# Activation tiles of a streaming encoder step at a pitch of 320 columns instead of 288, with six small buffers put into shared places

## The chip, the cores and the metric

The kernel runs on one core of one Trainium2 chip. The metric is the device time of one execution in microseconds (us). Smaller is better.

## The reference: what is computed

One layer of a streaming encoder for two request groups that share weights: a prompt of 256 tokens and a sample of 32 tokens with a cache of 128 past ones, 288 tokens in all. The model width is 2048, the FFN width 5504. Everything is float32.

```python
xp = xp + 0.5 * swiglu_ffn(xp, *ffn1)             # the same for the sample group, xs
op, sp = mixer_prompt(rmsnorm(xp, g1), *lw)       # z = h @ W_in, three attention groups, concat @ W_out
xp = xp + op
xp = xp + 0.5 * swiglu_ffn(xp, *ffn2)
# swiglu_ffn(x) = (silu(h @ w_gate) * (h @ w_up)) @ w_down, with h = rmsnorm(x, g)
```

The mixer's groups are A (12 heads over 4 key heads, the keys chosen by a lightning indexer: per query the top quarter of the keys by a weighted sum of relu(q_idx . k_idx)), B (10 heads over 2 key heads, window 128, sinks) and C (10 heads, clipped relative bias). Keys and values are also returned as caches.

## The kernel before, in words

**Tiling.** Activations lie transposed: 128 partitions carry 128 of the features, and the 288 tokens lie along the free dimension. A tile of 128 x 288 float32 is thus 1152 bytes in each partition. `h_hi` and `h_lo` (16 tiles each) hold the normalized input, `gu_hi` and `gu_lo` (15 tiles each) a third of the gated FFN values, `o_hi` and `o_lo` (16 tiles each, in the same place as `gu`, at another time) the attention output. These six are the "streamed" or right-side tensors: the moving operands of the large products.

**Precision.** Each float32 product is made of three products in the type float32r: `hi` and `lo` are the upper and the remaining part of a number, of activations as of weights. In `products` three matmuls per tile k go to one PSUM bank:

```python
pe.matmul(out, w_hi[b][:, k, :], hi, start=(k == first_k), stop=False)     # L594
pe.matmul(out, w_hi[b][:, k, :], lo, start=False, stop=False)              # L595
mm = pe.matmul(out, w_lo[b][:, k, :], hi, start=False, stop=(k == last_k)) # L596
```

Each of them also loads its 128 x 128 weight tile (LDWEIGHTS). A *strip* is all k of one output tile of 128 features.

**Phases.** `plan_phases` puts the strips in order. For each FFN, three times: *up* (30, 28 and 28 strips of 16 tiles; gate and up in turn) and *down* (16 strips of 15, 14 and 14 tiles). Between the two FFNs: *prep* (11 strips: index queries, keys and values), *cb* (20 strips with the attention of groups C and B between them), *a* (6 strips with attention A) and *wo* (16 strips). That makes 4,976 steps of k, so 14,928 large matmuls. All strips run one after another on TensorE. SyncE brings each strip's weights into `raw` (two buffers), ScalarE makes `w_hi` (L1049), VectorE makes `w_lo` (L1360), one strip ahead. VectorE reads the finished products from PSUM (L1384, L1720), ScalarE and VectorE make the next right side (L1266, L1685).

**Norms.** The sum of squares of x for an RMS norm is gathered in `sumsq` (VectorE, cleared at L1696, added to at L1367) from `sqx` (ScalarE, L1055), multiplied with a matrix of means (L641) and its root taken into `sd_x` (L1066). This happens three times: at the start, in the last *down* of the first FFN, and in *wo*.

**Attention buffers.** `kt_c` holds the keys of one pair of C heads (288 new, 128 cached): GpSimd places the cached ones (L1849), VectorE the new ones (L1414), GpSimd's queue stores the new ones to the output (L1898, L1899, semaphore `k_out`). `sq`, `z_k`, `p_t` serve attention too. `vec_t5` holds T5 bias vectors until they are stored in DRAM near the start. `idx_acc` holds the index sums for three blocks of queries.

**Places.** On-chip tensors lie one behind another in the order in which they are created. In the laid-out program before, these are the first bytes of a partition's share: `h_hi` 35,136 (137 x 256 + 64), `h_lo` 53,568 (209 x 256 + 64), `gu_hi` and `o_hi` 121,152 (473 x 256 + 64), `gu_lo` 138,432 (540 x 256 + 192), `o_lo` 139,584 (545 x 256 + 64). The weight tensors `w_hi` and `w_lo` all start at 64 past a multiple of 256, and their tiles are 512 bytes apart. As 1152 is 4.5 x 256, successive tiles of a right side lie alternately at 64 and at 192 past a multiple of 256.

Of the kernel before, what the change touches and what calls it, by code (L numbers as in the profile page):

```python
# [13 lines left out]
F32R = mybir.dt.float32r  # L14

P = 128
HD = 64
CHUNK = 64
H_A, KV_A, H_IDX, H_B, KV_B, H_C = 12, 4, 8, 10, 2, 10
# [6 lines left out]
VEC = 3 * P  # L26
# [87 lines left out]
def encoder_step(nc, x, cak, cav, caki, cbk, cbv, cck, ccv, w_in, w_out, qk_norm, sinks, c_bias, t5_bias,  # L114
                 w_gate, w_up, w_down, onehot,
                 yt, pak, pav, paki, pbk, pbv, pck, pcv, sak, sav, saki, sbk, sbv, sck, scv):
    T_P, T_S = pav.shape[2], sav.shape[2]
    D = w_out.shape[0]
    PAST = cav.shape[2]
    D_FF = w_gate.shape[1]  # L120
    NT = T_P + T_S
    DT, FT = D // P, D_FF // P
# [5 lines left out]
    thirds = [p.more["size"] for p in phases if p.name == "up"][:3]  # L128


    ctx = ExitStack()
    with ctx:
        def sb(name, shape, dt=F32, scope=ctx):
            return scope.enter_context(nc.sbuf_tensor(name, shape, dt))

        def sem(name):
            return ctx.enter_context(nc.semaphore(name))
# [2 lines left out]
        x_room = sb("gains_and_x", [P, 3 * DT + DT * NT])  # L140
        g_cols = x_room[:, 0:3 * DT]
        xT = x_room[:, 3 * DT:3 * DT + DT * NT].rearrange("p (k n) -> p k n", n=NT)
        h_hi = sb("h_hi", [P, DT, NT], F32R)
        h_lo = sb("h_lo", [P, DT, NT], F32R)
        raw = [sb(f"raw{s}", [P, 16, P]) for s in range(2)]
        w_hi = [sb(f"w_hi{s}", [P, 16, P], F32R) for s in range(2)]
        w_lo = [sb(f"w_lo{s}", [P, 16, P], F32R) for s in range(2)]
# [2 lines left out]
            below_second = sb("below_second", [P, 2, NT], F32, scope)  # L150
            raw_second = [sb(f"raw_second{s}", [P, 16, P], F32, scope) for s in range(2)]
        with ExitStack() as ffn_scope:
            gu_hi = sb("gu_hi", [P, thirds[0], NT], F32R, ffn_scope)
            gu_lo = sb("gu_lo", [P, thirds[0], NT], F32R, ffn_scope)
        o_hi = sb("o_hi", [P, 16, NT], F32R)
        o_lo = sb("o_lo", [P, 16, NT], F32R)

        ident = sb("ident", [P, P])
        mean_d = sb("mean_d", [P, P])
# [4 lines left out]
        sink_rows = sb("sink_rows", [P, 2, 5])  # L164
        neg_sinks = sb("neg_sinks", [P, 2, 5])
        rstd = sb("rstd", [P, NT])
        sumsq = sb("sumsq", [P, NT])
        sqx = sb("sqx", [P, NT])
        sd_x = sb("sd_x", [P, NT])
        table_first = sb("table_first", [P, 3])  # L170
        warm = gu_hi[:, 0:2, :].rearrange("p k n -> p (k n)")[:, 0:512]

        KEYS = T_P + PAST + T_S
        kt_a = sb("kt_a", [P, 2, KEYS])
# [20 lines left out]
        z_k = sb("z_k", [P, NT])  # L195
# [3 lines left out]
        sq = sb("sq", [P, NT])  # L199
# [2 lines left out]
        sq_wide = [sq_room[:, at:at + WIDE] for at in (0, NT, NT + WIDE)]  # L202
        sq_set = [t[:, 0:NT] for t in sq_wide]
        key_hi, key_lo = o_hi[:, 5, :], o_lo[:, 5, :]
        sd = sb("sd", [P, NT + 12])
        rinv = sb("rinv", [P, NT])
        v_c = sb("v_c", [P, 4, P])
        kt_c = sb("kt_c", [P, KEYS])
        vec_t5 = sb("vec_t5", [H_A + H_B, VEC])

        with ExitStack() as scope:
            t5_rows = sb("t5_rows", [T5_BUCKETS, H_A + H_B], F32, scope)
# [1 line left out]
        s_buf = [sb(f"s_buf{s}", [P, 2, T_P]) for s in range(2)]  # L214
        s_buf += [z_prep[:, 0:2, 0:T_P], z_prep[:, 2:4, 0:T_P]]
        p_t = [sb(f"p_t{r}", [P, 4, P]) for r in range(3)]
        bias_rev = [sb(f"bias_rev{s}", [P, 2, T_P]) for s in range(2)]
        idx_acc = [sb(f"idx_acc{r}", [P, n]) for r, n in enumerate((2 * P, P, PAST + T_S))]
        a_mask = [sb(f"a_mask{r}", [P, n]) for r, n in enumerate((2 * P, P, PAST + T_S))]
        nmax = [sb(f"nmax{s}", [P, 2]) for s in range(2)]  # L220
        snk = [sb(f"snk{s}", [P, 2]) for s in range(2)]
# [83 lines left out]
        k_out = sem("keys_stored")  # L305
# [16 lines left out]
        def x_piece(i):  # L322

            return [at for at, (s, _) in enumerate(FIRST) if s == 0].index(i)

        def first_no(i):

            return sum(k.stop < DT for _, k in FIRST[:i + 1])
# [99 lines left out]
        VOUT_PREP, KOUT_PREP = len(vout_no), len(kout_no)  # L428
# [587 lines left out]
        def _(act):  # L1016
# [114 lines left out]
            def prep_items(step):  # L1131
                for it in PREP_ITEMS.get(step, []):
                    if it[0] == "n":
                        z, done = {"ka0": (0, 6), "ka1": (1, 7), "kb": (8, 10)}[it[1]]
                        squares(z_prep[:, z, :], phase["prep"].n0 + done)
                        deviation(misc_no[it], norm_no[it])
                    elif it[0] == "v":
                        v, cols, _, _, _ = v_place(it[1])
                        place_v(misc_no[it], v, cols)
                    elif it[0] == "s":  # L1140
                        set_deviation(misc_no[it], 0, True, (0, 1))
                    elif it[0] == "w":
                        act.wait_ge(m_done, misc_no[it] + 1)
                        act.activation(w_tok[:, 0:2, :], misc_bank(misc_no[it])[:, 0:2 * H_IDX].rearrange("p (t c) -> p t c", t=2), ACT.Copy)
                        act.activation(w_tok[0:T_S, 2, :], misc_bank(misc_no[it])[0:T_S, 2 * H_IDX:3 * H_IDX], ACT.Copy).then_inc(m_free, 1)
                    elif it[0] == "i":
                        u = it[1]
                        r, _ = idx_units[u]
                        act.wait_ge(iq_done, u + 1)
                        if u >= 2:  # L1150
                            act.wait_ge(iacc, 2 * u - 2)
                        m, n = ROWS[r], NKEY[r]
                        for c in range(2):
                            a = act.activation(s_buf[u % 2][0:m, c, 0:n], psum[2 + u % 2 * 2 + c][0:m, 0:n], ACT.Relu)
                        a.then_inc(irelu, 1)
# [180 lines left out]
        def _(dve):  # L1336
            steps = [0]

            def link(ins):

                steps[0] += 1
                ins.then_inc(dve_link, 1)
                dve.wait_ge(dve_link, steps[0])
# [300 lines left out]
            for ph in phases:  # L1644
# [42 lines left out]
                elif ph.name in ("down", "wo"):  # L1687
# [5 lines left out]
                    if h_after:  # L1693

                        dve.wait_ge(m_done, [0, 1, 2][index])
                        link(dve.memset(sumsq[:, :], 0.0))  # L1696

                    final = ph.next is None
# [38 lines left out]
                elif ph.name == "prep":  # L1737
# [10 lines left out]
                    n = ph.n0 + 4  # L1748
# [275 lines left out]
```

## Time and profile before

| | |
|---|---|
| Time, median of 3 runs | 2085.09 us (2084.61 to 2085.61) |
| Span of the profiled execution | 2083.5 us (the page gives the span alone; the median of the timed runs is 1.6 us above it) |
| TensorE matmuls busy | 2077.8 us, 15,805 instructions |
| TensorE weight loads busy | 2057.7 us, 15,805 instructions |
| VectorE, ScalarE, GpSimd busy | 1169.9, 846.7, 88.8 us |
| Granted TensorE clock | 1.000 (mean) |

A matmul's duration in the profile is the time from its start to its modelled end, and it overlaps the next one; what a matmul costs is the distance from its start to the next one's start.

### The profile page before, as it was taken

How to read it: one execution, taken by the hardware profiler on the slowest of the kernel's cores; microseconds unless marked ns; L12 is line 12 of the kernel's file. 1: busy time of each engine (PE TensorE's matmuls, PEld its weight loads, DVE VectorE, ACT ScalarE, POOL GpSimd, SP SyncE). 2: the span in 40 equal slices, each digit the busy share in tenths (PEclk: the TensorE clock that was granted, in tenths of full speed). 3: DMA queues.
4: the chain of work that ended last, by engine and by line, in shares of the span. 5: the costliest groups of instructions: out<-in, count | busy, mean ns of one | idle time of the engine just before them, and what ended most of it. 6: DMA issues, size and time to landing. Idle time of an engine off the chain costs nothing.

```text
span 2083.5 us, 41883 instructions
## 1 busy us (share of the span) xinstructions
PE 2077.8 (100%) x15805; PEld 2057.7 (99%) x15805; DVE 1169.9 (56%) x1790; ACT 846.7 (41%) x1290; POOL 88.8 (4%) x140
## 2 busy tenths in 40 slices
PE   9999999999999999999999999999999999999999
PEld 8999999999999999999999999999999999999999
DVE  7554445554455556588879755555445554455544
ACT  6333333333333344345558544333333333333332
POOL 0000000000000000022432000000000000000000
PEclk9999999999999999999999999999999999999999
DMA  7444555444544545544443454544445444545554
GB/s 256 161 161 158 170 169 169 161 159 160 175 156 167 165 152 175 176 142 154 150 151 112 146 165 163 169 166 158 169 159 166 165 166 159 169 161 165 165 180 140
DMA packets 101274, 339.96 MB, mean 163 GB/s; under 512 B 12149, under 2 KB 16293, under 8 KB 101200
## 3 DMA queue, kind: packets, MB, share of 16 engines
q1 hardware_dynamic: 95856, 329.41, 47.7%
q0 software_dynamic: 2960, 7.45, 1.3%
q10 hardware_dynamic: 2400, 2.33, 0.3%
q8 instruction: 36, 0.59, 0.1%
q14 instruction: 22, 0.18, 0.0%
HBM read 334.45 MB, written 5.28 MB: 163 GB/s over the span
## 4 chain that ended last, share of the span: by engine, by line
PE 98%; DVE 1%; DMA 0%; ACT 0%; SPq 0%; issue 0%; DVEq 0%; ACTq 0%
PE bank L594 32%; PE bank L596 31%; PE bank L595 31%; PE bank L681 1%; PE bank L714 1%; PE bank L696 1%; PE bank L658 0%; DMA raw<-in_w_ffn_gate 0%; PE bank L896 0%; PE bank L698 0%; DVE w_lo L1360 0%; ACT w_hi L1049 0%; DVE rstd L1378 0%; PE bank L717 0%; PE bank L719 0%
## 5 line engine op out<-in xcount | busy, mean ns | idle before, releaser
L594 PE MATMUL bank<-h_hi,w_hi 128*128 128x288 f32 x3344 | 994.3, 297 | 0.9 <-DVE w_lo L1617 0.8
L595 PE MATMUL bank<-h_lo,w_hi 128*128 128x288 f32 x3344 | 986.5, 295 | 0.0
L596 PE MATMUL bank<-h_hi,w_lo 128*128 128x288 f32 x3344 | 983.3, 294 | 0.0
L1360 DVE TENSOR_TENSOR w_lo<-raw,w_hi 128x1024 fp32r<-128x1024 f32 x634 | 729.7, 1191 | 208.1 <-ACT w_hi L1049 207.6
L1049 ACT ACTIVATE w_hi<-raw 128x1024 fp32r<-128x1024 f32 x634 | 617.5, 1022 | 328.0 <-PE bank L596 325.5
L594 PEld LDWEIGHTS bank<-h_hi,w_hi 128*128 128x128 f32 x3344 | 626.7, 187 | 5.8 <-DVE w_lo L1617 2.1
L596 PEld LDWEIGHTS bank<-h_hi,w_lo 128*128 128x128 f32 x3344 | 629.8, 188 | 0.0
L595 PEld LDWEIGHTS bank<-h_lo,w_hi 128*128 128x128 f32 x3344 | 628.0, 188 | 0.2
L594 PE MATMUL bank<-gu_hi,w_hi 128*128 128x288 f32 x1376 | 407.0, 296 | 0.0
L595 PE MATMUL bank<-gu_lo,w_hi 128*128 128x288 f32 x1376 | 406.8, 296 | 0.0
L596 PE MATMUL bank<-gu_hi,w_lo 128*128 128x288 f32 x1376 | 406.4, 295 | 0.0
L596 PEld LDWEIGHTS bank<-gu_hi,w_lo 128*128 128x128 f32 x1376 | 259.6, 189 | 0.0
L595 PEld LDWEIGHTS bank<-gu_lo,w_hi 128*128 128x128 f32 x1376 | 259.6, 189 | 0.0
L594 PEld LDWEIGHTS bank<-gu_hi,w_hi 128*128 128x128 f32 x1376 | 259.4, 188 | 0.0
L1266 ACT ACTIVATE gu_hi<-gu 128x288 f32 (+1 forms) x86 | 38.2, 445 | 391.5 <-DVE gu L1682 391.5
L1720 DVE SCALAR_TENSOR_TENSOR gains_and_x<-bank,gains_and_x 128x288 f32 (+1 forms) x96 | 43.9, 457 | 201.4 <-PE bank L596 200.4
L1262 ACT ACTIVATE g_sig<-g_act 128x288 f32<-128x288 f32 x86 | 38.2, 444 | 283.9 <-DVE g_act L1384 283.9
L1384 DVE TENSOR_TENSOR u_act<-bank,rstd 128x288 f32<-128x288 f32 x86 | 39.3, 457 | 165.1 <-PE bank L596 165.0
L1384 DVE TENSOR_TENSOR g_act<-bank,rstd 128x288 f32<-128x288 f32 x86 | 39.4, 458 | 117.9 <-PE bank L596 117.8
L1685 DVE TENSOR_TENSOR gu_lo<-gu,gu_hi 128x288 f32 (+1 forms) x86 | 39.4, 458 | 67.8 <-ACT gu_hi L1266 67.8
L594 PE MATMUL bank<-o_hi,w_hi 128*128 128x288 f32 x256 | 75.9, 297 | 0.0
L595 PE MATMUL bank<-o_lo,w_hi 128*128 128x288 f32 x256 | 75.6, 295 | 0.0
(198 smaller groups left out, 985.8 us busy)
## 6 DMA issues: line engine op xcount, KB each, us to landing
raw<-in_w_ffn_gate SPq DMA_DIRECT2D x168, 512.0 KB, 4.5
raw<-in_w_ffn_up SPq DMA_DIRECT2D x168, 512.0 KB, 4.5
raw<-in_w_ffn_down SPq DMA_DIRECT2D x96, 512.0 KB, 3.7
raw<-in_w_in SPq DMA_DIRECT2D x74, 512.0 KB, 4.6
raw<-in_w_ffn_down SPq DMA_DIRECT2D x64, 384.0 KB, 4.2
raw<-in_w_out SPq DMA_DIRECT2D x32, 512.0 KB, 4.5
raw<-in_w_ffn_down SPq DMA_DIRECT2D x32, 448.0 KB, 4.3
bias_rev<-bias_vectors POOLq DMA_DIRECT2D x11, 256.0 KB, 4.6
```

Source lines behind the costliest of these rows:

```text
L594: pe.matmul(out, w_hi[b][:, k, :], hi, start=(k == first_k), stop=False)
L595: pe.matmul(out, w_hi[b][:, k, :], lo, start=False, stop=False)
L596: mm = pe.matmul(out, w_lo[b][:, k, :], hi, start=False, stop=(k == last_k))
L681: mm = pe.matmul(bank_s[c][:, b * T_P:b * T_P + NKEY[r]], q[half, FULL[r]], kt[half, KEY0[r]:KEY0[r] + NKEY[r]], start=True, stop=True)
L696: mm = pe.transpose(bank_t[b][:, o:o + P], s_buf[slot][:, c, kc * P:(kc + 1) * P], ident[:, :])
L1049: act.activation(w_hi[b][:, k, :], raw_tile(ph, j, s)[:, k, :], ACT.Copy).then_inc(hi_rdy, 1)
L1262: act.activation(g_sig[:, :], g_act[:, :], ACT.Silu).then_inc(sig_rdy, 1)
L1266: act.activation(gu_hi[:, j, :], gu[:, :], ACT.Copy).then_inc(guh_rdy, 1)
L1360: dve.tensor_tensor(w_lo[b][:, k, :], raw_tile(ph, j, s)[:, k, :], w_hi[b][:, k, :].bitcast(F32), ALU.subtract)\
L1384: return dve.tensor_tensor(dst, (early_bank(n) or bank_w[b])[rows, cols], rstd[rows, cols], ALU.mult)
L1685: dve.tensor_tensor(gu_lo[:, j, :], gu[:, :], gu_hi[:, j, :].bitcast(F32), ALU.subtract).then_inc(gul_rdy, 1)
L1720: dve.scalar_tensor_tensor(dst, src[:, 0:NT], factor, xT[:, d, :], ALU.mult, ALU.add)\
```

## The change

The right sides get a pitch of `TILE = -(-NT // 64) * 64`, that is 320 columns (1280 bytes) instead of 288. The matmuls still read 288 columns each, and columns 288 to 319 of a tile are never read by a product. This takes 8,192 bytes more of each partition. Room comes from putting other buffers together: `sqx` becomes `sq`, `sd_x` becomes `z_k`, `sumsq` becomes the first 288 columns of `kt_c`, `vec_t5` a part of `p_t[1]`, and the first two `idx_acc` parts of `p_t[0]` (6,528 bytes less). One wait is added: before `sumsq` is cleared in *wo*, VectorE waits until all stores of keys have landed. No instruction is added or removed otherwise, and the instructions' order stays.

```diff
+        def right_side(name, tiles, scope=ctx):
+            room = sb(name, [P, tiles, TILE], F32R, scope)
+            return room[:, :, 0:NT], room
+
+        TILE = -(-NT // 64) * 64
-        h_hi = sb("h_hi", [P, DT, NT], F32R)
-        h_lo = sb("h_lo", [P, DT, NT], F32R)
+        h_hi, _ = right_side("h_hi", DT)
+        h_lo, _ = right_side("h_lo", DT)
...
-            gu_hi = sb("gu_hi", [P, thirds[0], NT], F32R, ffn_scope)
-            gu_lo = sb("gu_lo", [P, thirds[0], NT], F32R, ffn_scope)
-        o_hi = sb("o_hi", [P, 16, NT], F32R)
-        o_lo = sb("o_lo", [P, 16, NT], F32R)
+            gu_hi, gu_room = right_side("gu_hi", thirds[0], ffn_scope)
+            gu_lo, _ = right_side("gu_lo", thirds[0], ffn_scope)
+        o_hi, _ = right_side("o_hi", 16)
+        o_lo, _ = right_side("o_lo", 16)
...
-        sumsq = sb("sumsq", [P, NT])
-        sqx = sb("sqx", [P, NT])
-        sd_x = sb("sd_x", [P, NT])
-        warm = gu_hi[:, 0:2, :].rearrange("p k n -> p (k n)")[:, 0:512]
+        warm = gu_room[:, 0:2, :].rearrange("p k n -> p (k n)")[:, 0:512]
...
+        sqx = sq
+        sd_x = z_k
-        vec_t5 = sb("vec_t5", [H_A + H_B, VEC])
+        sumsq = kt_c[:, 0:NT]
...
+        vec_t5 = p_t[1][0:H_A + H_B, 0:VEC // P, :].rearrange("p k n -> p (k n)")
+        first_rows = p_t[0][:, 0:3, :].rearrange("p k n -> p (k n)")
-        idx_acc = [sb(f"idx_acc{r}", [P, n]) for r, n in enumerate((2 * P, P, PAST + T_S))]
+        idx_acc = [first_rows[:, 0:2 * P], first_rows[:, 2 * P:3 * P], sb("idx_acc2", [P, PAST + T_S])]
...
                         dve.wait_ge(m_done, [0, 1, 2][index])
+                        if ph.name == "wo":
+                            dve.wait_ge(k_out, 32 * (KOUT_PREP + 5))
                         link(dve.memset(sumsq[:, :], 0.0))
```

## Rows read from the trace of the kernel before

**Rows 1.** The page's first part: busy time by engine.
```profile
PE 2077.8 (100%) x15805; PEld 2057.7 (99%) x15805; DVE 1169.9 (56%) x1790; ACT 846.7 (41%) x1290; POOL 88.8 (4%) x140
```
**Rows 2.** The waits of TensorE: total us, times, longest.
```profile
PE bank L905 <- DVE gu_hi L1594: 1.7, 1, 1.7
PE bank L594 <- DVE w_lo L1617: 0.8, 2, 0.6
PE bank L698 <- DVE z_prep L1477: 0.2, 1, 0.2
```
**Rows 3.** Windows of six phases: length, PE busy (instructions), clock, DMA share, GB/s.
```profile
202.40:298.10 95.70, 95.70 (x723) 1.00 0.50 167
298.10:477.30 179.20, 179.20 (x1347) 1.00 0.49 162
477.30:566.90 89.60, 89.60 (x674) 1.00 0.50 167
...
1447.70:1543.40 95.70, 95.70 (x723) 1.00 0.50 166
...
1812.10:1991.30 179.20, 179.20 (x1346) 1.00 0.49 163
1991.30:2080.80 89.50, 89.50 (x672) 1.00 0.50 166
```
**Rows 4.** Timeline of TensorE in an up phase: start us, us, instruction.
```profile
599.78 0.29 PE L594 MATMUL bank<-h_hi,w_hi 128*128 128x288 f32 x1
599.91 0.29 PE L595 MATMUL bank<-h_lo,w_hi 128*128 128x288 f32 x1
600.05 0.29 PE L596 MATMUL bank<-h_hi,w_lo 128*128 128x288 f32 x1
600.18 0.30 PE L594 MATMUL bank<-h_hi,w_hi 128*128 128x288 f32 x1
...
600.58 0.29 PE L594 MATMUL bank<-h_hi,w_hi 128*128 128x288 f32 x1
...
600.98 0.30 PE L594 MATMUL bank<-h_hi,w_hi 128*128 128x288 f32 x1
...
603.78 0.29 PE L594 MATMUL bank<-h_hi,w_hi 128*128 128x288 f32 x1
```
**Rows 5.** The same in a down phase.
```profile
499.78 0.30 PE L594 MATMUL bank<-gu_hi,w_hi 128*128 128x288 f32 x1
...
500.31 0.30 PE L595 MATMUL bank<-gu_lo,w_hi 128*128 128x288 f32 x1
500.45 0.29 PE L596 MATMUL bank<-gu_hi,w_lo 128*128 128x288 f32 x1
500.59 0.29 PE L594 MATMUL bank<-gu_hi,w_hi 128*128 128x288 f32 x1
...
502.19 0.29 PE L594 MATMUL bank<-gu_hi,w_hi 128*128 128x288 f32 x1
```
**Rows 6.** The tile mean_d: duration ns min/median/max, first and last start us.
```profile
L641 PE MATMUL bank<-sumsq,mean_d x6: 405/406/406, 34.9 to 1261.6; 128*128 128x288 f32 x6
```
**Rows 7.** Timeline of TensorE around the first norm product.
```profile
34.87 0.65 PE L641 MATMUL bank<-sumsq,mean_d 128*128 128x288 f32 x2
```
**Rows 8.** The tiles kt_c and sumsq: durations as above, first and last start.
```profile
L1849 POOL COPY kt_c<-kc_cache x5: 422/2304/2462, 858.5 to 1075.4; 128x128 f32 x3, 128x128 f32<-128x128 f32 x2
L1899 POOL DMA_DIRECT2D out<-kt_c x5: 537/540/540, 959.4 to 1088.9; - x5
...
DMA to landing us min/median/max: 4.7/5.0/5.5
...
L1696 DVE MEMSET sumsq<- x2: 298/298/298, 748.0 to 1168.1; 128x288 f32 x2
```

## The prediction

> **What bounds the kernel now.** I began with busy time by engine [rows 1]: TensorE is busy for 2077.8 of the 2083.5 us of the span, VectorE for 56% of it, ScalarE for 41%. A busy share of 100% doesn't prove a bound, since matmuls overlap in this view, so I went on to TensorE's waits [rows 2]: they sum to 2.7 us in the whole span. Neither weights, nor right sides, nor free banks come late, apart from the first 50 us. Only two things can then move the time: the distance between starts of the 14,928 large matmuls, or a new wait long enough to reach TensorE.
>
> The windows by phase give that distance [rows 3]. An up phase of 28 strips has 28 x 16 x 3 = 1344 large matmuls and takes 179.2 us: 133.3 ns each (the two or three further instructions in the row's count are neighbours cut by the window's ends). A down phase with 14 tiles has 672 and takes 89.6 us: again 133.3. A down phase with 15 tiles has 720 and takes 95.7 us: 132.9. The second FFN's rows repeat this. So 14,928 x 133.3 ns = 1,990 us of the span is this one number. The other 93 us are start, attention and end.
>
> At the full clock, 288 columns at one per 2.4 GHz cycle are 120 ns; the row's 133.3 ns are 320 cycles. That 13.3 ns are missing, and that 320 is the new pitch, makes one suspicious that the chip charges for a rounded-up tile. The question of the case is whether the place of a tile decides this.
>
> **The change part by part.** *The pitch.* Every large matmul still reads 288 columns and its own weight tile, so no work goes away by count. What changes is the place at which a read starts. Before, tiles lie alternately 64 and 192 bytes past a multiple of 256. With 1280 = 5 x 256 every tile keeps the place of its tensor's first one. The added bytes ahead of each tensor (2,048 for each of `h_hi` and `h_lo`, so 4,096 before `gu` and `o`) are multiples of 256. So `h_hi`, `h_lo`, `gu_hi`, `o_hi` and `o_lo` start at 64 past as before, and `gu_lo`, behind 15 x 1280 = 19,200 bytes = 75 x 256, moves from 192 to 64. After the change all tiles lie at 64 past a multiple of 256. None lies on a multiple of 128 or of 256, neither before nor after. The change makes the places equal; it doesn't align them.
>
> And 64 past is not a new place: half of the tiles have it before. If it were cheaper or dearer than 192 past, the trace would show it. In an up phase all three matmuls of a tile k read from one kind of place, the next three from the other. The starts of L594 lie 0.40 us apart from tile to tile: 599.78, 600.18, 600.58, 600.98, and ten tiles after the first 603.78, which is 4.00 us later [rows 4]. No two neighbours differ by more than the row's rounding of 0.01 us, which is 3 ns for one matmul. In a down phase hi and lo of a tile lie at different places, so that the places alternate from one matmul to the next; there too six tiles take 502.19 - 499.78 = 2.41 us, 133.9 ns for one, and the phase's mean is 133.3 [rows 5, 3]. Triples in turn or one by one, the mean is the same 133.3. The 16 tiles also cover every place of the form 64 + 128 j within 2,048 bytes, so every place that a tile takes at the new pitch, seen modulo 2,048, was taken before by some tile at that price. I take 0 for a matmul's change in cost. The bounds: from below the rate of the plain float32 product of the same 288 columns. Its two instructions span 0.65 us from the first one's start to the second one's end [rows 7], and one takes 406 ns [rows 6], so they start 0.24 us apart; if the float32 instruction counts as two passes over the columns, a pass costs 120 ns, 13 ns less than a large matmul. From above the longest steady distance that rows show, 0.14 us (500.31 to 500.45 to 500.59) [rows 5], is 6.7 ns more.
>
> A rule of the Trainium skill bears on the size. "TensorE: Matmul & The Clock Gate", section "Back-to-back issue gap", gives N / 2.4 + 2.5 ns for a warm matmul, 122.5 ns for 288 columns; the trace shows 133.3, so the rule is off by 10.8 ns here, or something in this kernel costs that much. By the rule the sum would be 14,928 x 10.8 = 161 us lower, if the change removed what is over.
>
> *The irregular phases.* The two 15-tile down phases are 0.3 us each under the 133.3 of the rest (96.0 - 95.7) [rows 3]. In them a strip has an odd number of matmuls, so the alternation of places is broken once a strip. With one kind of place nothing alternates, and I assume that these two go to 133.3 as well: +0.6 us. The bounds are 0 and the same sum with a gain in all phases, which is 14,928 x 0.43 ns = 6.4 us less.
>
> *The added wait.* VectorE waits for the stores of `kt_c` before it clears `sumsq` in wo. The last such store is issued at 1088.9 and takes about 5.0 us to land, until 1094; the clearing starts at 1168.1 [rows 8]. The wait ends 74 us before it is reached: 0 us, unless stores slip by that much. If they did, every VectorE instruction behind it would wait, `w_lo` of the coming strips first, and TensorE two strips later.
>
> *The shared places.* Sharing could only cost through waits, and the diff adds none but that one; orders and counts of all other instructions stay. `sumsq` in `kt_c` is used up to the start of prep (phase end near 835.6), and the cached keys are first placed there at 858.5 [rows 8]. `sqx`, `sd_x`, `vec_t5` and `idx_acc` keep their instructions. VectorE and ScalarE do the same shapes, and even some per cent on them would vanish behind TensorE, with 56% and 41% busy [rows 1]. The stores of y at the end come from the same tiles. 0 us.
>
> Sum against the profiled span: 2083.5 + 0 + 0.6 + 0 + 0 = 2084.1; the runs' median is 1.6 us above the span, so 2085.7 us.
>
> **The rivals.** *Alignment pays after all (faster).* The 13.3 ns over 120 would be a cost of reads from alternating places, and with equal places each matmul would run at the pass rate of the norm product: 14,928 x 13.3 = 199 us less, 1887 us. For it speaks that 320 cycles fit a rounding so well. Against it speak the even distances in rows 4: within three matmuls of one place nothing is gained, and the alternating down phase costs no more than the triples. If it holds only in part, by what the 15-tile strips show, 6 us less. The skill's 122.5 ns would give 2085 - 161 = 1924 us by this mechanism.
>
> *Equal places collide (slower).* Weight tiles lie at 64 past a multiple of 256 too, and a weight load runs beside each matmul. Now both kinds of reads are in step always, before it was every second one. If that costs, each large matmul would go to the 0.14 us that some have in rows 5: 14,928 x 6.7 ns = 100 us more, 2185 us. It decides from 0.3 ns a matmul (4 us in all). Against it: the tiles already in step cost no more than the others [rows 4].
>
> *The change doesn't do what it says.* As an alignment to 256 bytes it doesn't, since all bases are 64 past; that is my forecast's ground rather than a rival. If the alignment is meant to be to 64 columns of the tensor, it does, and nothing follows.
>
> *The wait holds VectorE (slower).* Were the stores 80 us late, the time would grow by about 6 us, 2092 us. Nothing in rows 8 hints at it.
>
> **How the numbers follow.** About 0.2% (4.2 us) is what a measurement of this kernel tells from no change. No change, with up to a microsecond either way: 0.79. The two faster cases together 0.13: alignment pays in full or in a large part 0.09 (the equal distances speak clearly against it, but that 320 cycles appear without an explanation leaves it some), a few us from regular spacing 0.04. Slower 0.08: collision 0.06, wait or something that I don't see 0.02. Without the rivals the time lies from 2084 to 2087. The range for 8 in 10 takes in the bound of the irregular phases, 6 us less, and as much of the slower side as the wait's price: 2079 to 2092.
>
> **What would show it.** Right: an up phase of 28 strips still takes 179.2 us and L594 starts every 0.40 us; the clearing at L1696 starts near 1168 with no wait ahead of it; the 15-tile down phases take 95.7 to 96.0 us. Wrong for the pitch: up phases at 161 to 165 us (distance 120 to 122.5 ns) or above 180 us. Then the argument that failed would be that equal distances in the trace before mean equal cost by place: starts could be evened out by something that I take for the array's own rate. Wrong for the shares: a wait of VectorE ahead of L1696, or new waits of TensorE on `w_lo`.

## The result, and the profile after

The changed kernel takes 2062.55 us in the median of 4 runs (2062.3 to 2065.46, the last at a granted clock of 0.998) against 2085.05 us before: a ratio of 0.9894, 95% interval 0.9879 to 0.9908. It is 1.1% faster. The prediction said no change (2085.7 us, range 2079 to 2092), so it was wrong.

The windows of the changed kernel over the phases that [rows 3] show of before (length, TensorE busy and its instructions, clock, DMA share, GB/s):

```profile
202.20:297.00 94.80, 94.80 (x722) 1.00 0.52 169
297.00:474.00 177.00, 177.00 (x1347) 1.00 0.50 164
474.00:562.40 88.40, 88.40 (x674) 1.00 0.52 168
1434.10:1528.90 94.80, 94.80 (x722) 1.00 0.51 168
1794.40:1971.40 177.00, 177.00 (x1347) 1.00 0.51 166
```

The counts are the same, the windows are shorter: an up phase of 1344 large matmuls takes 177.0 instead of 179.2 us, a down phase of 672 takes 88.4 instead of 89.6, one of 720 takes 94.8 instead of 95.7. In all of them a large matmul now costs 131.7 ns (94.8 / 720), where it cost 133.3, or 132.9 in the 15-tile phases. TensorE's timeline in an up phase (start us, us, instruction) against [rows 4]:

```profile
599.85 0.30 PE L600 MATMUL bank<-h_hi,w_hi 128*128 128x288 f32 x1
...
600.25 0.29 PE L600 MATMUL bank<-h_hi,w_hi 128*128 128x288 f32 x1
...
600.64 0.29 PE L600 MATMUL bank<-h_hi,w_hi 128*128 128x288 f32 x1
...
603.80 0.29 PE L600 MATMUL bank<-h_hi,w_hi 128*128 128x288 f32 x1
```

Ten tiles take 3.95 us, before it was 4.00. That is the whole gain: 1.67 ns in each large matmul. Over 14,928 that would be 24.9 us. The median fell by 22.5. The 15-tile phases had been at 132.9 already, so each gained 0.9 us and not 1.2. By the starts of their matmuls, the first phase gained 1.8 us where its count times 1.67 ns is 2.4, and prep to *wo* gained 3.4 of 4.2. Part of that is the *wo* phase, which had not been at 133.3 before either. A window of 80 us inside it has two more matmuls in the kernel before,

```profile
1170.00:1250.00 80.00, 80.00 (x604) 1.00 0.49 162
```

than in a kernel that runs *wo* at 133.3 ns (the second experiment below):

```profile
1170.00:1250.00 80.00, 80.00 (x602) 1.00 0.50 159
```

Measured from start to start, the *wo* phase before has 132.9 ns a matmul.

The waits of TensorE (total us, times, longest), against [rows 2]:

```profile
PE bank L911 <- DVE gu_hi L1600: 1.7, 1, 1.7
PE bank L600 <- DVE w_lo L1623: 0.9, 1, 0.9
PE bank L704 <- DVE z_prep L1483: 0.4, 1, 0.4
```

No wait has come or gone there; the largest change is 0.2 us. The tile `kt_c`, in which `sumsq` lies now, against [rows 8]:

```profile
L1907 POOL DMA_DIRECT2D out<-kt_c x5: 537/537/540, 949.1 to 1077.4; - x5
...
L1704 DVE MEMSET kt_c<- x2: 298/298/298, 740.0 to 1156.4; 128x288 f32 x2
```

The last store is issued at 1077.4 and lands about 5 us later; the clearing that has the added wait runs at 1156.4. The wait was over long before it was reached, as the prediction had it.

### The profile page after: what moved, and what is told of

Same layout as the page of the kernel before. It is cut to its first block, busy times and chain, and to the rows that moved or that the text cites. A ratio compares the mean times of both kernels' runs of the same rounds, so it can differ in the third digit from the quotient of the medians.

```text
span 2060.9 us, 41883 instructions
## 1 busy us (share of the span) xinstructions
PE 2054.7 (100%) x15805; PEld 2034.4 (99%) x15805; DVE 1170.6 (57%) x1790; ACT 846.4 (41%) x1290; POOL 88.5 (4%) x140
## 4 chain that ended last, share of the span: by engine, by line
PE 97%; DVE 1%; ACT 1%; issue 0%; DMA 0%; SPq 0%; DVEq 0%; ACTq 0%
PE bank L600 32%; PE bank L601 31%; PE bank L602 31%; PE bank L687 1%; PE bank L720 1%; PE bank L702 1%; PE bank L664 0%; DMA raw<-in_w_ffn_gate 0%; DVE w_lo L1366 0%; PE bank L902 0%; ACT w_hi L1055 0%; ACT s_buf L1112 0%; PE bank L704 0%; DVE z_prep L1447 0%; ACT z_prep L1112 0%
```

## The experiments

The expectations name the theories: by theory 1 the right sides' own place sets the price, by theory 2 it is enough that all their places are equal, by theory 3 their place relative to the weight tiles counts. Most runs move places alone; three load or multiply less, and one sets the pitch back. `wfirst` stands for this edit of the changed kernel: the tensors `raw`, `w_hi`, `w_lo` are created ahead of the right sides, with a gap of a few columns ahead of or behind them, so that the places of both groups can be chosen. A place is given as bytes past a multiple of 256. *Distance* is the right sides' place minus the weights', modulo 256. `raw` always moves together with `w_hi` and `w_lo`, so these runs don't separate it from them.

```diff
         x_room = sb("gains_and_x", [P, 3 * DT + DT * NT])
+        sb("gap_w", [P, A])            # moves weights and right sides by 4 A bytes
+        raw = ...; w_hi = ...; w_lo = ...
+        sb("gap_m", [P, B])            # moves the right sides by 4 B bytes
...
         h_hi, _ = right_side("h_hi", DT)
         h_lo, _ = right_side("h_lo", DT)
-        raw = ...; w_hi = ...; w_lo = ...
```

One measure serves all runs: the matmuls counted in the window from 302 to 470 us, which lies inside one up phase in each kernel. (Only in the three that leave work out does it reach into the next down phase; there the pace is the same.) The window plus the 0.3 us of a matmul that crosses its end, 168.3 us, divided by the count is the distance between starts, the *pace*. One matmul more or less in the count moves it by 0.1 ns, so that 1262 and 1263 are the same pace. It is written as 133.3 ns, which the starts themselves give. Before and after give the scale:

```profile
302.00:470.00 168.00, 168.00 (x1262) 1.00 0.49 162
```

is the kernel before, 133.3 ns, and

```profile
302.00:470.00 168.00, 168.00 (x1278) 1.00 0.50 164
```

the changed one, 131.7 ns.

**Right sides moved to 0** (A = 0, B = 48; weights at 64). 

> The changed kernel, with every right-side tile at a multiple of 256 bytes (gap of 192 bytes ahead of them), weights left at 64 past. In the changed kernel a large matmul costs 131.67 ns. Theory 1, a tile's own start modulo 256 sets the price (64 past: 131.67; 192 past: 135.0, mean 133.33): a start on a multiple is another price, and if fewer touched blocks are cheaper it is at most 131.67, perhaps down to 120 to 122.5 ns, 1887 to 1930 us. Theory 2, only that successive reads start in equal places counts: 131.67 ns, 2062.5 us. Theory 3, being in step with the weight tiles (both 64 past) is the cheap case: no longer in step, so 133.3 to 135 ns, 2085 to 2112 us.

```profile
302.00:470.00 168.00, 168.00 (x1263) 1.00 0.49 162
```

2086.53 us (8 runs; ratio to before 1.0006, interval 0.9995 to 1.0018), pace 133.3 ns. All tiles on multiples of 256, all in equal places, and the gain is gone. This refutes that equal places are enough, and that aligning the right sides to 256 bytes by itself helps.

**Right sides at 192** (A = 0, B = 32). 

> The changed kernel, with every right-side tile at 192 bytes past a multiple of 256, weights left at 64 past. Theory 1 (own start modulo 256): 135.0 ns a matmul, that is 14,928 x 3.33 ns = 50 us over the changed kernel, 2112 us. Theory 2 (equal places are enough): 131.67 ns and 2062.5 us. Theory 3 (in step with the weights): out of step, 2085 to 2112 us.

```profile
302.00:470.00 168.00, 168.00 (x1262) 1.00 0.50 162
```

2086.51 us, ratio 1.0007 (0.9996 to 1.0018), 133.3 ns. Equal places fail again; theory 1 had said 135.0 ns, which isn't reached either.

**Right sides and weights at 0** (A = 48, B = 0). 

> The changed kernel with right-side tiles and weight tiles all on multiples of 256 bytes. Theory 1: the same as with the right sides alone moved there. Theory 2: 131.67 ns, 2062.5 us. Theory 3: in step again, 131.67 ns, 2062.5 us, where the run with the right sides alone moved is slower.

```profile
302.00:470.00 168.00, 168.00 (x1278) 1.00 0.50 165
```

2063.39 us (2 runs), ratio 0.9897 (0.9868 to 0.9926), 131.7 ns. Against the first run only the place of the weights (with `raw`) differs, and the gain is back. The distance to the weights counts.

**Pitch 288, begun at 0** (the kernel before, `wfirst` with B = 48: distances 192 and 64 in turn). 

> The kernel before, pitch 288, but the right sides begin on a multiple of 256 bytes, so that their tiles lie at 0 and 128 past in turn instead of 64 and 192; weights at 64 past. Theory 1: the mean of the prices of 0 and of 128 past; unlike 133.33 ns and below it if starts on multiples of 128 are cheap, time below 2085 us. Theory 2 (only equal places help): 133.33 ns and 2085 us, as before. Theory 3: neither place is in step, so 133.3 ns or more, 2085 us or more.

```profile
302.00:470.00 168.00, 168.00 (x1273) 1.00 0.50 164
```

2070.53 us (3 runs), ratio 0.993 (0.9907 to 0.9952), 132.2 ns. No theory had this: 0.7% faster than before, at the old pitch.

**Three further distances: 64, 32, 96** (right sides at 128, 96, 160; B = 16, 8, 24). 

> The changed kernel with right-side tiles at 128 past a multiple of 256, weights at 64 past: 64 bytes ahead of the weights. Theory 3 (the distance between a tile's place and the weights' place, modulo 256, sets the price; so far 0: 131.67 ns, 128 and 192: 133.33 ns): pitch 288 with distances 64 and 192 in turn gave 132.2 ns, so if prices average, 64 costs 131.1 ns and this kernel takes 2054 us. Theory 2' (only two prices, 131.67 for in step, 133.33 for anything else): 133.33 ns, 2086.5 us.

 

> Right-side tiles at 96 past, 32 bytes ahead of the weights' place. Theory 3, price a smooth or stepped function of the distance: between those of distance 0 and 64, 131.1 to 131.7 ns, 2054 to 2063 us. Theory 2' (in step or not): 133.33 ns, 2086.5 us. If a start that is no multiple of 64 bytes costs by itself, more than that.

 

> Right-side tiles at 160 past, 96 bytes ahead of the weights' place. Theory 3: between the prices of distance 64 (131.1 if prices average) and 128 (133.33 ns), so 2054 to 2086 us. Theory 2': 133.33 ns, 2086.5 us.

 In this order:

```profile
302.00:470.00 168.00, 168.00 (x1273) 1.00 0.50 164
```

```profile
302.00:470.00 168.00, 168.00 (x1262) 1.00 0.49 162
```

```profile
302.00:470.00 168.00, 168.00 (x1278) 1.00 0.49 164
1170.00:1250.00 80.00, 80.00 (x603) 1.00 0.50 164
```

Distance 64: 2065.68 us (3 runs, 2062.66 to 2069.48), 132.2 ns in this execution. Distance 32: 2086.35 us (8 runs), 133.3 ns. Distance 96: 2064.35 us (2 runs), 131.7 ns. The price is no smooth function of the distance: 32 lies between two cheap ones and is dear. The second row of the last fence is a window in the wo phase of the same execution. The changed kernel has 608 matmuls in it:

```profile
1170.00:1250.00 80.00, 80.00 (x608) 1.00 0.51 168
```

At distance 96 it has 603, the count of a dear distance (602 with the right sides at 192), although the places are the same as in the up phase. So at one distance two paces are possible. Start by start, the trace shows 133.3 ns through the whole wo phase, and 131.7 in the phases before and after it. In the execution at distance 64 the pace is 131.7 ns from 838 to 864 us (prep) and 132.2 from 51 to 832 us. Both times it changed only where other matmuls had interrupted the stream. The spread of the three runs at distance 64, 0.3% where the kernel before keeps within 0.1% at a granted clock of 1.000, would fit executions that differ in this; only one of the three has a trace.

**The shared places and the wait alone.** 

> The changed kernel with TILE = 288: the shared places and the added wait alone, pitch and places of the right sides as before. All theories of the place of tiles: 133.33 ns and 2085 us. A theory in which the shared buffers or the shifted small ones bring the gain: near 2062.5 us.

```diff
-        TILE = -(-NT // 64) * 64
+        TILE = NT
```

```profile
302.00:470.00 168.00, 168.00 (x1262) 1.00 0.49 162
```

2084.86 us (8 runs), ratio 1.0001 (0.999 to 1.0012). Sharing, the wait and the shifted small buffers do nothing; they pay for the room alone.

**Two of three weight loads halved.** That is a third less loaded in all. 

> The changed kernel, but two of each three large matmuls (hi x w_hi except for the first k, and lo x w_hi) load and use only 64 of the 128 weight columns; they still stream 288 columns of activations. It leaves out those products for the upper 64 output features of each strip. Theory A, the weight load that runs beside a matmul takes reading slots from its moving operand: the time over 120 ns shrinks with the load, by half where all loads are halved, so the mean distance falls from 131.7 to some 128 ns. Theory B, the 11.7 ns over 120 are a fixed cost of each matmul: 131.7 ns stays.

```diff
-                    pe.matmul(out, w_hi[b][:, k, :], hi, start=(k == first_k), stop=False)
-                    pe.matmul(out, w_hi[b][:, k, :], lo, start=False, stop=False)
+                    m = P if k == first_k else 64
+                    pe.matmul(out[0:m], w_hi[b][:, k, 0:m], hi, start=(k == first_k), stop=False)
+                    pe.matmul(out[0:64], w_hi[b][:, k, 0:64], lo, start=False, stop=False)
```

```profile
302.00:470.00 168.00, 168.00 (x1284) 1.00 0.50 162
```

2053.55 us (1 run), pace 131.1 ns. It is the lowest pace of all kernels that stream 288 columns, but only 0.6 ns under the changed kernel; theory A had 128. Most of what is above 120 ns (the estimate for one pass, from the norm product in the prediction) isn't in proportion to the load.

**272 columns in two of three.** 

> The changed kernel, but the second and third matmul of each three stream 272 columns instead of 288; it leaves out the lo products for the last 16 tokens. Theory A (288 cycles of streaming plus a term for the weight load): 16 columns less are 6.7 ns less for two of three, so the mean distance is 131.7 - 4.4 = 127.2 ns. Rival C (a read is charged in blocks of 64 columns, 5 blocks = 320 columns): 272 columns from 16 past still touch the same 5 blocks, so the distance stays at 131.7 ns.

```diff
-                    pe.matmul(out, w_hi[b][:, k, :], lo, start=False, stop=False)
-                    mm = pe.matmul(out, w_lo[b][:, k, :], hi, start=False, stop=(k == last_k))
+                    pe.matmul(out[:, 0:272], w_hi[b][:, k, :], lo[:, 0:272], start=False, stop=False)
+                    mm = pe.matmul(out[:, 0:272], w_lo[b][:, k, :], hi[:, 0:272], start=False, stop=(k == last_k))
```

```profile
302.00:470.00 168.00, 168.00 (x1306) 1.00 0.51 168
```

2021.32 us (1 run), mean pace 128.9 ns. Three matmuls take 386.7 ns instead of 395.0, so 8.3 ns less, where 32 columns at the estimate of 120 ns for 288 are 13.3 ns. Blocks of 64 columns (rival C, no gain) are refuted, so that 320 cycles equal 5 x 64 explains nothing here. Theory A's plain sum (127.2) isn't met either.

**Only the weights moved.** Right sides stay at 64 as in the changed kernel, weights at 192 (A = 32, B = 32) and at 0 (A = 48, B = 16). 

> The changed kernel with the right sides left at 64 past a multiple of 256 and the weight tensors moved to 192 past. Theory 3 (the distance between both places counts): distance 128, as in the run with the right sides at 192 and weights at 64: 133.33 ns and 2086.5 us. Theory 1 (a right side's own place counts): nothing that it names has changed, 131.67 ns and 2062.5 us.

 

> The changed kernel with the right sides left at 64 past and the weight tensors at 0 past: distance 64, as in the run with right sides at 128 and weights at 64, which had 132.2 ns in most phases and 131.67 in prep. Theory 3: 131.67 to 132.2 ns, 2063 to 2070 us. If the places count one by one as well, another value.

 In this order:

```profile
302.00:470.00 168.00, 168.00 (x1262) 1.00 0.49 162
```

```profile
302.00:470.00 168.00, 168.00 (x1272) 1.00 0.50 164
```

Weights at 192, distance 128: 2086.06 us, ratio 1.0002 (0.9991 to 1.0014), 133.3 ns. Nothing about the right sides differs from the changed kernel, and its gain is gone. The two gaps make 256 bytes together, so every tensor behind them keeps its place modulo 256 too; only `raw`, `w_hi` and `w_lo` have another. Weights at 0, distance 64: 2069.22 us (2 runs), 0.9923 (0.9894 to 0.9952), 132.3 ns, as at distance 64 with both groups elsewhere. At distances 0, 64 and 128 the same distance gave the same pace from other places.

**The two distances left, 160 and 224** (right sides at 224 and at 32; B = 40, 56). 

> The changed kernel with right sides at 224 past a multiple of 256, weights at 64: distance 160. Theory 3 with the distances so far (0: 131.67 ns; 32: 133.33; 64: 132.22; 96: 131.67; 128: 133.33; 192: 133.33) gives no rule for 160; between its neighbours 128 and 192 it would be 133.33 ns and 2086 us. If the price is a pattern that repeats every 128 (0 against 128 already speaks against that), it would be that of 32, 133.33 ns.

 

> Right sides at 32 past, weights at 64: distance 224. Between the neighbours 192 (133.33 ns) and 0 (131.67 ns): 131.7 to 133.3 ns, 2062 to 2086 us. Theory 2' (only equal places are cheap) is already contradicted by 64 and 96.

 In this order:

```profile
302.00:470.00 168.00, 168.00 (x1262) 1.00 0.50 162
```

```profile
302.00:470.00 168.00, 168.00 (x1262) 1.00 0.49 162
```

2086.35 and 2085.87 us (1 run each), both 133.3 ns.

**The halved loads at a bad distance.** The edit of the halved loads, with right sides at 192 and weights at 64. 

> Right sides at 192 past, weights at 64 (distance 128, 133.33 ns with whole loads), and two of three weight loads and matmuls use only 64 weight columns, as in the run with half weights at distance 0, which had 131.11 ns. It leaves out the upper 64 output features of those products. Theory A (reads of the weight load hinder the reads of the stream): with half the load reads, most of what the bad distance costs goes too, so between 131.1 and 132.2 ns. Theory B (the distance acts without the load's reads, for instance through the start of each matmul alone): the whole difference of 1.67 ns stays, 132.8 ns.

```profile
302.00:470.00 168.00, 168.00 (x1284) 1.00 0.50 163
```

2053.76 us (1 run), 131.1 ns, the same as at distance 0. With whole loads the two distances are 1.67 ns a matmul and 24 us apart, with halved loads 0.2 us. So the distance acts through the loads, as far as one run each and two distances show it. The halved matmuls also write only 64 output rows, which this edit doesn't separate from the loads; but the runs with only the weights moved point to the loads as well, since on TensorE nothing else reads `w_hi` and `w_lo`.

**Pitch 288 at distances 96 and 224 in turn** (kernel before, B = 24). 

> The kernel before (pitch 288) with right sides beginning at 160 past and weights at 64 past: distances 96 and 224 in turn, no added memory for tiles. If prices average: (131.67 + that of 224) / 2, so 131.7 to 132.5 ns, 2062 to 2074 us. If the dearer of both sets the pace, as 0 and 128 in turn did (133.33, not 132.5 ns): the price of 224.

```profile
302.00:470.00 168.00, 168.00 (x1273) 1.00 0.50 163
```

2075.04 us (4 runs), ratio 0.9953 (0.9933 to 0.9972), 132.2 ns here. Cheaper than before, dearer than begun at 0, and a window in a down phase says why:

```profile
480.00:560.00 80.00, 80.00 (x602) 1.00 0.54 170
```

is this kernel, at 133.3 ns there, and

```profile
480.00:560.00 80.00, 80.00 (x608) 1.00 0.53 174
```

the one begun at 0, at 132.2. All six down phases, 4128 matmuls, are 1.1 ns dearer, which makes 4.5 us, as much as the two medians differ by. Both phases of this kernel use the distances 96 and 224. In the up phases hi and lo of a tile have the same one, so three matmuls in a row share it; in the down phases it changes from one matmul to the next. So besides the distances their order can count.

**Whether VectorE and ScalarE are the partner.** They write `w_lo` and `w_hi`, so a collision of their writes with TensorE's reads would depend on places too. The traces speak against it. In the kernel before, three matmuls (from L594 to L594, in the window above) take 400.0 ns in the 81 cases in which neither engine is busy, and 400.0 in the 338 others. With the right sides at 0 it is 400.0 and 400.0 again, with them at 128 it is 396.7 and 396.7, and in the changed kernel 394.3 and 395.2.

## Why the prediction was wrong, point by point

**What bounds the kernel: right.** The distance between starts of the large matmuls was the only number that mattered, and the waits stayed where they were.

**The step that failed: "If it were cheaper or dearer than 192 past, the trace would show it."** From this step came the term that was wrong, "I take 0 for a matmul's change in cost"; it measured -1.67 ns in the phases that had been at 133.3. The step read the even distances of [rows 4] as equal prices of both places, and priced the change of pitch at 0. The rows are right and the inference is wrong. With both places in turn, the kernel before runs at one pace of 133.3 ns for all, which is the pace of a distance of 128 taken alone. With one of these places alone, distance 0, it runs at 131.7, though that place too is "not a new place" and had been "taken before by some tile at that price". The pace in a mixed stream belongs to the stream, not to the tile. The starts, read to the nanosecond in that window, show the same for streams of one place. Before, they lie 132 to 134 ns apart; in the changed kernel about every fourth distance is 126 or 127 and the others 132 to 135; with the right sides at 0 it is 130 and 136 or 137 in turn, though every read starts at the same distance. Each pace is the mean of a pattern over several matmuls. The prediction named this weakness among what would prove it wrong ("starts could be evened out") and gave it too little. Its signs for a wrong pitch term, up phases at 161 to 165 us or above 180, didn't have the 177.0 us that came either.

**The missing partner.** The argument looked for an effect of a tile's own start. The run with only the weights moved shows that this isn't the quantity: the right sides stayed where the changed kernel has them, and the time went from 2062.55 to 2086.06 us. The slower rival, "equal places collide", had the right partner, the weight load beside each matmul, and the opposite sign: in step is cheap, at both places where it was tried (2062.55 and 2063.39 us).

**The faster rival** had the right sign and the wrong size and cause: 1887 us for alignment to the full, 2079 for the part that the 15-tile strips suggest. On multiples of 256 with the weights left alone nothing was gained. The 122.5 ns by the formula of the Trainium skill ("TensorE: Matmul & The Clock Gate", section "Back-to-back issue gap"), which that section calls the gap of an isolated matmul, are reached in none of the runs with 288 columns; the lowest pace is 131.1 ns.

**The irregular phases.** +0.6 us was assumed, -1.8 us came (95.7 to 94.8, twice). That they ran under 133.3 before was a hint that this pace is no floor, and the prediction used it only as a bound of 6 us. Its reason for them, a broken alternation, can't be the only one: the wo phase has 48 matmuls in a strip, an even number, and ran at 132.9 before too.

**The wait and the shares: right.** 0 us; the run with these alone is at 1.0001 of before.

**What is shown, what stays open.** Shown: the gain comes from the pitch; it depends on the distance modulo 256 between right sides and weight tiles; with halved loads the dependence is gone at the two distances tried. By distance the pace was 131.7 ns at 0 (in every uninterrupted phase of both kernels), 133.3 at 32, 132.2 at 64 (131.7 in prep, in one of two traces), 131.7 at 96 (133.3 in one phase), 133.3 at 128, 160, 192 and 224. Open: which mechanism inside makes this list; why 0 and 128 in turn run at the dearer's pace, while 64 and 192 in turn, and 96 and 224 in the up phases, run at 132.2, under the dearer's own; what decides which of two paces a phase keeps; and what the 11.7 ns above 120 are that remain at the best distance. A conflict between two read streams whose timing locks into one of several patterns would fit, and the repeating patterns of starts speak for it, but that it is a conflict of reads is argued, not shown. The DMA's writes into `raw` were not varied by themselves; they went on in the runs with halved loads, where the dependence was gone. Within the places tried, no version beat the changed kernel clearly; the one with everything on multiples of 256 equals it.

## What to carry to other kernels

In a stream of matmuls that each load their own weights, the start of the moving tile relative to the start of the weight tile is a free parameter. It was worth about 1% here, for float32r operands and 288 columns, the only case measured. Give all moving tiles one place modulo 256 bytes, the same as the weight tiles', and check the pace by counting matmuls in a fixed window. Aligning the moving tiles by themselves can miss it altogether, and a cheap distance in one phase can be dear in another, so count in each phase. And an even spacing in a trace of mixed cases doesn't prove that the cases cost the same; only a stream of one case alone does.

## What the runs showed of the hardware

The pace moved though nothing but the places in the instructions differed: the same 14,928 large matmuls at a granted clock of 1.00 took 133.3 or 131.7 ns each by a shift of 128 bytes of one group of tensors against another. This doesn't fit what the Trainium skill says. "TensorE: Matmul & The Clock Gate", section "Part 2: What happens when you issue a matmul", has two independent read ports, so that loading the next weights takes no read bandwidth from the running matmul. Here the pace depends on where the loads read relative to the stream, and halving two of three loads takes that dependence away (131.1 ns at distances 0 and 128); the measurement decides, at least for float32r operands of 288 columns.

Also not expected: one kernel can run its phases at different paces in one execution (distance 96: 1278 matmuls in 168 us of an up phase as in the best case, but 603 in 80 us of wo as in the worst; the kernel before had 133.3 ns in its up phases and 132.9 in wo, with the same places). Executions of one kernel can differ by more than others do (2062.66 to 2069.48 us at distance 64), perhaps for that reason.
